# A two-block transformer on one core: cross-attention scored from the PSUM bank for all four heads, the next phase's preparation one slot later, and the constants loaded later

## The reference

```
x = x + 0.5 * swiglu(rms_norm(x, ffn1_norm), gate, up, down)        # width 5632
x = x + hybrid_mixer(rms_norm(x, mix_norm), ...)                    # dilated attention, gated linear attention
q = rms_norm(heads(rms_norm(x, xattn_norm) @ w_q), q_norm)          # 4 heads of 128
k = rms_norm(heads(rms_norm(mem, mem_norm) @ w_k), k_norm)
v = heads(rms_norm(mem, mem_norm) @ w_v)
p = softmax((q @ k.T) * 128 ** -0.5)
x = x + heads_joined(p @ v) @ w_o
x = x + 0.5 * swiglu(rms_norm(x, ffn2_norm), ...)
# second block: a recurrent layer (RG-LRU and HGRN2), then a layer of differential attention
```

## Time and profile before

| | |
|---|---|
| median of 3 runs | 3620.53 us (3617.46 to 3620.82) |
| the profiled execution | 3612.52 us |
| its span, first to last instruction | 3610.7 us |
| mean granted clock of PE | 0.985 |
| PE busy | 3465.4 us, 96% |
| DVE, ACT, POOL busy | 63%, 47%, 11% |
| DMA | 592.35 MB, 164 GB/s in the mean |

### The profile page before, as it was taken

The page is one execution under the profiler, slowest core; times in us unless marked ns, Lnnn a source line. Parts: engine busy times, 40 slices in busy tenths (PEclk is TensorE's granted clock), DMA queues, the critical chain, the costliest instruction groups (busy, mean ns, idle before and its releaser), DMA issues.

```text
span 3610.7 us, 59062 instructions
## 1 busy us (share of the span) xinstructions
PE 3465.4 (96%) x19584; PEld 2984.7 (83%) x19584; DVE 2291.8 (63%) x3508; ACT 1711.8 (47%) x2446; POOL 393.7 (11%) x442
## 2 busy tenths in 40 slices
PE   8999999988999998999999989999999989999999
PEld 7888888867787877888888878878888878888878
DVE  6666666655665655666666657765666656666665
ACT  5444444444443554444444446754444435444443
POOL 1000000011122201000000011210333421101010
PEclk9999999999999999999999999999999999999999
DMA  6565555543443543666555554555444435444435
GB/s 225 186 186 186 186 186 186 165 143 123 137 154 116 191 153 123 186 186 186 186 186 186 182 163 162 188 161 181 152 147 149 146 117 175 145 151 140 147 126 169
DMA packets 167920, 592.35 MB, mean 164 GB/s; under 512 B 18320, under 2 KB 22672, under 8 KB 167712
## 3 DMA queue, kind: packets, MB, share of 16 engines
q1 hardware_dynamic: 166688, 587.11, 51.6%
q10 hardware_dynamic: 1152, 4.19, 0.3%
HBM read 589.14 MB, written 2.10 MB: 164 GB/s over the span
## 4 chain that ended last, share of the span: by engine, by line
PE 47%; issue 13%; DVE 4%; ACT 2%; POOL 2%; ACTq 0%; DVEq 0%; POOLq 0%
PE bank L383 26%; PE bank L384 13%; PE bank L574 2%; PE bank L381 2%; DVE w_low L1210 1%; ACT w_high L808 1%; PE bank L380 1%; PE bank L588 1%; POOL work L1790 1%; DVE normed L1255 1%; POOL rstd L1742 1%; DVE residual L1245 0%; PE bank L466 0%; DVE increment L1242 0%; PE bank L473 0%
## 5 line engine op out<-in xcount | busy, mean ns | idle before, releaser
L383 PE MATMUL bank<-normed,w_high 128*128 128x512 f32 x5820 | 2124.2, 406 | 15.1 <-DVE w_low L1210 9.9
L1210 DVE TENSOR_TENSOR w_low<-w_raw,w_high 128x1024 fp32r<-128x1024 f32 (+1 forms) x1120 | 1366.5, 1230 | 678.8 <-ACT w_high L808 656.6
L384 PE MATMUL bank<-normed,w_low 128*128 128x256 f32 x5820 | 1641.2, 282 | 0.0
L808 ACT ACTIVATE w_high<-w_raw 128x1024 fp32r<-128x1024 f32 (+1 forms) x1120 | 1161.3, 1043 | 695.1 <-PE bank L384 669.7
L383 PEld LDWEIGHTS bank<-normed,w_high 128*128 128x128 f32 x5820 | 1104.7, 190 | 272.3 <-issue 17.8
L384 PEld LDWEIGHTS bank<-normed,w_low 128*128 128x128 f32 x5820 | 1110.0, 191 | 21.0 <-issue 7.7
L383 PE MATMUL bank<-mixed,w_high 128*128 128x512 f32 x2268 | 815.1, 401 | 31.9 <-DVE increment L1242 19.1
L384 PE MATMUL bank<-mixed,w_low 128*128 128x256 f32 x2268 | 638.6, 282 | 0.0
L383 PEld LDWEIGHTS bank<-mixed,w_high 128*128 128x128 f32 x2268 | 428.9, 189 | 137.7 <-DVE increment L1242 24.0
L825 ACT ACTIVATE parts<-bank 128x256 f32<-128x256 f32 x456 | 174.0, 382 | 760.0 <-PE bank L381 759.4
L384 PEld LDWEIGHTS bank<-mixed,w_low 128*128 128x128 f32 x2268 | 431.0, 190 | 7.7 <-issue 0.5
(11 more groups left out here) (242 smaller groups left out, 2408.7 us busy)
## 6 DMA issues: line engine op xcount, KB each, us to landing
w_raw<-w_hg SPq DMA_DIRECT2D x128, 512.0 KB, 3.5
w_raw<-w_att SPq DMA_DIRECT2D x128, 512.0 KB, 3.5
w_raw<-w_up1a SPq DMA_DIRECT2D x64, 512.0 KB, 4.2
w_raw<-w_up1b SPq DMA_DIRECT2D x64, 512.0 KB, 4.1
w_raw<-w_up2a SPq DMA_DIRECT2D x64, 512.0 KB, 4.1
w_raw<-w_up2b SPq DMA_DIRECT2D x64, 512.0 KB, 4.2
w_raw<-w_rg SPq DMA_DIRECT2D x64, 512.0 KB, 3.6
w_raw<-w_up1c SPq DMA_DIRECT2D x48, 512.0 KB, 3.8
```

The costliest lines, as they stand in the source:

```text
L383: nc.tensor.matmul(banks[b][:, :], hi, x, start=starts and k == 0, stop=False)
L384: last = nc.tensor.matmul(banks[b][:, 0:S], lo, x[:, 0:S], start=False, stop=False)
L808: A_(wh[slot][:, 0:width], raw[slot][:, 0:width], ACT.Copy).then_inc(wh_done, 1)
L1210: TT(wl[slot][:, 0:width], raw[slot][:, 0:width], wh[slot][:, 0:width].bitcast(F32), ALU.subtract).then_inc(wl_done, 1)
```

## The change

In cross-attention all four scores are made before unit 3 of memv, each in a bank of its own; maximum and exponential read the bank, the query's factor goes into the exponential's scale, and `smooth` is gone. Transposes and products use more banks. The keys' eight diagonals are made in one go, in front of two spreads before unit 6. xo's first unit waits for the heads one by one. In down phases ACT's `high` and `square_tile` stand one slot later, behind the next split and copy, and DVE's `low` at j = 0 and 1 of the next body. In the four openings sum, diagonals and spread come one unit later. The constants are loaded after unit 7, masks and gate weights at dn1a.

```diff
@@ -141,13 +141,15 @@
+probs = (C[:, 0:2, :], C[:, 2:4, :], A[:, 0:2, :], A[:, 2:4, :])
+mem_diag = [diag[:, :], sq[:, 0:2, :].rearrange("p t s -> p (t s)")]
+scores, mixes = (p_a, p_b, p_bc, p_o), (p_bc, p_o, p_t, p_sum)
@@ -335,11 +338,14 @@
-            sp.dma_start(con[:, :], t_in["con"]).then_inc(loaded, 16)
+            for s in range(RING):
+                load(1, s, src[RING + s], width)
+            sp.dma_start(con[:, :], t_in["con"]).then_inc(con_in, 16)
+            first = 2
-            sp.dma_start(level_mask[:, :, :], t_in["masks"]).then_inc(loaded, 16)
...
+        elif name == "dn1a":
+            sp.dma_start(level_mask[:, :, :], t_in["masks"]).then_inc(loaded, 16)
...
@@ -390,6 +396,8 @@
         for t in range(UT):
+            if n + t // 4 == 0:
+                pe.wait_ge(crs["stored"], k + 1)
@@ -455,9 +463,9 @@
         if name in PREPARES.values():
-            if j == 1:
+            if j == 2:
                 sum_squares(name)
-            if j == 2:
+            if j == 3:
                 spread(rms, NORMED[name], S)
@@ -676,24 +684,21 @@
-            if hd >= 2:
-                pe.wait_ge(crs["smoothed"], hd - 1)
             for b in range(NB):
-                last = nc.tensor.matmul((p_a, p_b)[hd % 2][:, b * S:(b + 1) * S], Dm[:, hd, b * P:(b + 1) * P],
+                last = nc.tensor.matmul(scores[hd][:, b * S:(b + 1) * S], Dm[:, hd, b * P:(b + 1) * P],
         def turn(hd):
-            if hd:
-                pe.wait_ge(crs["copied"], hd)
+            if hd >= 2:
+                pe.wait_ge(crs["copied"], hd - 1)
                 for b in range(NB):
-                    last = nc.tensor.transpose(p_t[:, c * P:(c + 1) * P],
-                                               C[:, 2 * (hd % 2) + b, kb * P:(kb + 1) * P], C_("ident"))
+                    last = nc.tensor.transpose((p_t, p_sum)[hd % 2][:, c * P:(c + 1) * P],
+                                               probs[hd][:, b, kb * P:(kb + 1) * P], C_("ident"))
@@ -711,11 +716,11 @@
-            if j == 5:
-                spread(mem, 0, 2 * S)
             if j == 6:
-                pe.wait_ge(mem["keyed"], 1)
-                spread(mem, 1, 2 * S)
+                pe.wait_ge(mem["diagonal"], 1)
+                for r in range(2):
+                    nc.tensor.matmul((p_bc, p_o)[r][:, :], ones[:, :], mem_diag[r], start=True,
+                                     stop=True).then_inc(mem["spread"], 1)
@@ -726,31 +731,19 @@
             if j == 3:
-                score(0)
-                score(1)
-            if j == 5:
-                score(2)
-            if j == 6:
-                turn(0)
-                score(3)
-            if j == 7:
-                turn(1)
+                for hd in range(HEADS_X):
+                    score(hd)
+            if j >= 6:
+                turn(2 * j - 12)
+                turn(2 * j - 11)
+        pe.wait_ge(mem["valued"], 2)
         for hd in range(HEADS_X):
-            if hd < 2:
-                turn(hd + 2)
-            if hd == 0:
-                pe.wait_ge(mem["valued"], 2)
-            if hd == 2:
-                pe.wait_ge(crs["smoothed"], HEADS_X)
-            out_ = (p_o, p_bc, p_a, p_b)[hd]
             for kb in range(NB):
-                last = nc.tensor.matmul(out_[:, 0:S], VX[:, hd, kb, :], PX[hd][:, 2 * kb:2 * kb + 2, :],
+                last = nc.tensor.matmul(mixes[hd][:, 0:S], VX[:, hd, kb, :], PX[hd][:, 2 * kb:2 * kb + 2, :],
-        pe.wait_ge(crs["stored"], HEADS_X)
@@ -1005,23 +999,29 @@
             for j in range(RING):
+                if name in SQUARES and j == 0 and not (isinstance(i, int) and i == 0):
+                    added_tile(name, i * 2 - 1, 1)
                 if j >= 2:
-                    n = i * 2 + (j - 2)
-                    if name in SQUARES:
-                        act.wait_ge(x_done, n + (added(name) - KD + 1))
-                    if name in PREPARES:
-                        high(PREPARES[name], n, x_tile(n))
-                    if name in SQUARES:
-                        square_tile(SQUARES[name], n, j - 2, 2, x_tile(n))
+                if name in SQUARES and j == 3:
+                    added_tile(name, i * 2, 0)
 ...
+        if name in SQUARES:
+            added_tile(name, KD - 1, 1)
+    def added_tile(name, n, at_):
+        act.wait_ge(x_done, n + (added(name) - KD + 1))
+        if name in PREPARES:
+            high(PREPARES[name], n, x_tile(n))
+        square_tile(SQUARES[name], n, at_, 2, x_tile(n))
@@ -1035,29 +1035,17 @@
         def power(hd):
-            h2 = 2 * (hd % 2)
             for b in range(NB):
-                last = A_(C[:, h2 + b, :], C[:, h2 + b, :], ACT.Exp, bias=stat[:, 4 + h2 + b:5 + h2 + b],
-                          accum_out=stat[:, 8 + h2 + b:9 + h2 + b])
+                c = 2 * hd + b
+                last = A_(probs[hd][:, b, :], scores[hd][:, b * S:(b + 1) * S], ACT.Exp,
+                          bias=stat[:, 8 + c:9 + c], scale=rstd_q[:, c:c + 1], accum_out=stat[:, 16 + c:17 + c])
-        def smooth(hd):
-            act.wait_ge(crs["scored"], hd + 1)
-            if hd == 0:
-                act.wait_ge(crs["rooted"], 1)
-            if hd >= 2:
-                act.wait_ge(crs["transposed"], hd - 1)
-            for b in range(NB):
-                last = A_(C[:, 2 * (hd % 2) + b, :], (p_a, p_b)[hd % 2][:, b * S:(b + 1) * S], ACT.Copy,
-                          scale=rstd_q[:, 2 * hd + b:2 * hd + b + 1])
-            last.then_inc(crs["smoothed"], 1)
         def copy_probs(hd):
-            A_(PX[hd], p_t[:, :], ACT.Copy).then_inc(crs["copied"], 1)
+            A_(PX[hd], (p_t, p_sum)[hd % 2][:, :], ACT.Copy).then_inc(crs["copied"], 1)
@@ -1090,29 +1078,18 @@
-            if j == 3:
-                smooth(0)
-                smooth(1)
-            if j == 4:
-                power(0)
-                power(1)
-            if j == 5:
-                smooth(2)
-            if j == 6:
-                copy_probs(0)
-                smooth(3)
-                power(2)
-            if j == 7:
-                copy_probs(1)
-                power(3)
-        copy_probs(2)
+            if j in (4, 5):
+                power(2 * j - 8)
+                power(2 * j - 7)
+            if j >= 6:
+                copy_probs(2 * j - 12)
+                copy_probs(2 * j - 11)
-        copy_probs(3)
@@ -1271,10 +1248,8 @@
             for j in range(RING):
-                if to and j == 0 and not (isinstance(i, int) and i == 0):
-                    low(to, i * 2 - 1, x_tile(i * 2 - 1))
-                if to and j == 3:
-                    low(to, i * 2, x_tile(i * 2))
+                if to and j < 2 and not (isinstance(i, int) and i == 0):
+                    low(to, i * 2 - 2 + j, x_tile(i * 2 - 2 + j))
@@ -1286,6 +1261,7 @@
         if to:
+            low(to, KD - 2, x_tile(KD - 2))
@@ -1481,7 +1457,7 @@
-                    if opens and j == 0:
+                    if opens and j == 1:
                         factors(name)
@@ -1508,24 +1484,28 @@
         def largest(hd):
-            h2 = 2 * (hd % 2)
-            dve.wait_ge(crs["smoothed"], hd + 1)
-            own.did(nc.vector.reduce_max(stat[:, h2:h2 + 2], C[:, h2:h2 + 2, :], AX.X))
-            own.settle()
-            TS(stat[:, 4 + h2:6 + h2], stat[:, h2:h2 + 2], -1.0, None, ALU.mult).then_inc(crs["maxed"], 1)
+            c = 2 * hd
+            dve.wait_ge(crs["scored"], hd + 1)
+            own.did(nc.vector.reduce_max(stat[:, c:c + 2], scores[hd].rearrange("p (b s) -> p b s", b=NB), AX.X))
+            if hd == 0:
+                dve.wait_ge(crs["rooted"], 1)
+            own.settle()
+            STT(out=stat[:, 8 + c:10 + c], in0=stat[:, c:c + 2], scalar=-1.0, in1=rstd_q[:, c:c + 2],
+                op0=ALU.mult, op1=ALU.mult).then_inc(crs["maxed"], 1)
         def weigh(hd):
-            own.did(nc.vector.reciprocal(stat[:, 12 + h2:14 + h2], stat[:, 8 + h2:10 + h2]))
+            own.did(nc.vector.reciprocal(stat[:, 24 + c:26 + c], stat[:, 16 + c:18 + c]))
             for b in range(NB):
-                last = TS(C[:, h2 + b, :], C[:, h2 + b, :], stat[:, 12 + h2 + b:13 + h2 + b], None, ALU.mult)
+                last = TS(probs[hd][:, b, :], probs[hd][:, b, :], stat[:, 24 + c + b:25 + c + b], None, ALU.mult)
@@ -1552,36 +1532,31 @@
-            if j == 4:
-                diagonals(mem, 0, 0, 0, 4)
             if j == 5:
-                keys(0)
-                diagonals(mem, 1, 0, 4, 4)
-            if j == 6:
-                keys(1)
+                dve.wait_ge(mem["rooted"], 1)
+                for c in range(8):
+                    last = TS(mem_diag[c // 4][:, c % 4 * P:(c % 4 + 1) * P], C_("ident"), rstd[:, c:c + 1],
+                              None, ALU.mult)
+                last.then_inc(mem["diagonal"], 1)
+            if j >= 6:
+                keys(j - 6)
-            if j == 3:
-                largest(0)
-                largest(1)
-            if j == 4:
-                weigh(0)
```

(13 more changed lines are left out.)

36 lines of the change are left out of this document (19 added, 17 removed).

## The result

The changed kernel takes 3561.9 us (median of 4 runs, 3556.6 to 3571.2), the kernel before, measured beside it, 3619.1: ratio 0.9845, 95% interval 0.9823 to 0.9866. Measured again with more runs the two medians were 3564.0 and 3617.4 us (ratio 0.9855, 0.9835 to 0.9874).

What follows compares the result with a forecast made beforehand. PE, busy 96% of the span, bounds the kernel, so only its idle and half-speed time can be won. Terms sum to 43.6 us: 3612.5 becomes 3568.9, plus the median's 8 us gives 3577 us, range 3566 to 3591.

Steps and rivals of the forecast that it cites:

- Down phases, -19.1 us: In dn1c, dn2c and wout: all 16 PE waits for the second increment go, 19.1 us.
- In dn1c a matmul costs 68.37 / 379 = 0.18 us of busy time: Step pricing slow stretches from dn1c: twelve matmuls at half speed take 3.40 us instead of 2.2, losing 1.2 us.
- no such wait: 0: In rouB, with 8-tile units: no wait for the increment, so no gain was counted.
- Openings, -11.2 us, -0.2 and the new wait: mixa, up2a, rg, att: four sum waits go (11.2 us); rg's diagonal wait shrinks 0.2 to 3.3; mixa gains 0.9.
- the first rival: Openings' waits return one slot later because diagonals are late behind DVE's extra split; 3594 us, chance 0.12.
- Cross-attention, -5.1 us: Waits shrink in memk by 0.8 us, in xq by 2.2, in memv by 2.1; no clock gain taken.
- Start, -2.8 us: Later constants cut PE's 3.23 us start wait by 1.6 us and remove a slow stretch worth 1.2.
- DVE's two slowed splits (4.16 us) shift with ACT: At the start: DVE's two splits move earlier along with ACT, whose 1.55 us wait for weights goes whole.
- The clock, -7.3 us: Slow stretches won back: 6.1 us in the openings of mixa, up2a, att and rg, 1.2 at the start.
- The sum of 46.5 us: Alternative total gain if a 3.4 us slow stretch costs the skill's 1.7 us; 46.5 instead of 43.6, time 3574 us.
- The median of the runs is 8 us above that execution, and I keep this distance.: Whole kernel: 8 us between profiled execution and median of runs, carried over from 3568.9 to forecast 3577 us.
- The other rivals: Cross-attention gives nothing (0.10), 3582 us; clock does not return (0.06), 3584; down phases still wait (0.03), 3596; slower (0.03), 3630.

## Why the prediction missed, point by point

**Down phases, -19.1 us.** Right in mechanism and in time: all 16 waits went, and copy and increment stand within 0.1 us of where the prediction put them. What was mis-sized is the price of a wait. The step that failed is "In dn1c a matmul costs 68.37 / 379 = 0.18 us of busy time", with 8.7 us for a body and the gain counted as idle time alone. PE's busy time was taken as fixed work. It holds 0.22 to 0.27 us for every wait, so it falls when waits go. The four runs with waits of 0.7, 1.05 and 1.4 us in two stages show it as a price for each interruption. For the whole kernel: busy time fell by 4.3 us although the time at half speed rose from 110 to 121 us; at the fit's 0.35 us for each of these the fall would have been 8.0 us, and in the same way it is about 8 us in the second pair of profiles and in the down phases alone. Some 8 us of the gain were left out of the sum, 1.5 of them in rouB, of which the prediction says "no such wait: 0".

**Openings, -11.2 us, -0.2 and the new wait.** The waits went, and 3.78 in rg and 0.94 in mixa are near the 3.3 and 0.9 forecast. The credit is shared, though: with the down phases' order alone mixa's wait falls to 0.4 us, and with the later unit alone other waits take its place. Waits that return one slot later are what the first rival described; with the openings alone they do, but because the increments and squares are still late, and not for DVE's extra split that the rival named. Not foreseen was the slow stretch behind the 0.94 us: the stage takes 37.8 to 39.2 us in the four profiles that have it, against 36.6 with mixa's old units.

**Cross-attention, -5.1 us.** Right: 5.3 us of idle time against 4.3 forecast, 6.8 us in the runs. The second spread of xq, the wait ahead of unit 6, and nothing at xo's first unit all came as said. memk's 0.8 us was 0.3.

**Start, -2.8 us.** 3.6 us in the runs, with an interval from 0.4 to 7; by the rows PE goes on 1.4 us earlier, with 1.2 us less of wait, and a slow stretch in fewer profiles. The step "DVE's two slowed splits (4.16 us) shift with ACT" held nearly; they were 0.3 us slower still.

**The clock, -7.3 us.** The stages named got their stretches back, but for the start in both profiles of the changed kernel, and mixa got one of 6.8 us in another place. Their price was too low. The same stage at the same waits with more or less slow time: xq 51.9, 53.5 and 55.0 us with 0, 3.4 and 6.8 at half speed, the heads of att 525.7, 527.2 and 529.3 with 20.5, 23.9 and 27.3. That is 1.5 to 2.1 us for a stretch of 3.4, and not 1.2; at the end of hg, where PE waits for POOL in any case, it is 6.1 for 23.9, or 0.9. By the Trainium skill (TensorE: Matmul & The Clock Gate, "HAM oscillation — how this bites in real kernels") half of a slow stretch's length is lost, an estimate of 1.7 us for one of 3.4: xq and the heads of att agree with it nearly. The prediction's 1.2 came from counting 12 matmuls in 3.40 us. The order of time in that stretch gives more:

```profile
781.43 0.40 PE L383 MATMUL bank<-normed,w_high 128*128 128x512 f32 x1
781.78 0.39 PE L383 MATMUL bank<-normed,w_high 128*128 128x512 f32 x1
...
782.70 0.63 PE L383 MATMUL bank<-normed,w_high 128*128 128x512 f32 x1
783.34 0.63 PE L383 MATMUL bank<-normed,w_high 128*128 128x512 f32 x1
```

A pair of matmuls, one of L383 and one of L384, takes 0.35 us at 1.00 and 0.64 at 0.50, so 3.40 us hold 10.6 and lose 1.5 us. That it is less than half "since weight loads share PE's time" is argued in the prediction, and no run tests it. The sum of 46.5 us was the better one.

**"The median of the runs is 8 us above that execution, and I keep this distance."** This step failed too. The distance was the fortune of one execution and of a median of three; between the two profiles of that kernel the end of hg differs by 6.1 us, and other stages by up to 2.4, some the other way. The median of the kernel before is 3617.4 us over 29 runs, 3 us below the number that the forecast started from, and the first profiled execution after lies 9 us above its own median.

Put together: 36.5 us of waits (forecast 36.3), 8 of interruptions (0), and 0.0033 of mean clock, which at 1.9 us for each 0.001 (the table of 29 runs) is 6 us (7.3). That gives 50.8 of the 53.4 us between the means. The last 2 to 3 us are not settled: the profiled executions, two of each kernel, differ by 45.4 us, so most of the clock's share fell in executions without a trace. In which stages it lies there is not shown. That the waits' sum came out to 0.2 us is partly luck: start and memk gave 1.4 us less of idle time than said, and 1.5 us went at the end of hg and 0.5 in rouB, where nothing was forecast.

The other rivals did not come: the kernel is not slower, the down phases do not wait, DVE's low parts delay no split that PE waits for, and cross-attention gives its share.

## What to carry to other kernels

A wait costs its idle time and the interruption: compare the same matmuls with and without it, since busy time is not the work. Take the baseline from the median of many runs, look at the clock of the one that was profiled, and compare a stage only with the same stage at the same slow time. When two edits attack one lateness, as the squares' order and the unit at which their sum is asked, run each alone before a gain is credited to either; and when one engine's order is changed, what another engine waits for in the old place has to move with it.
